# Low parts of the weights by accumulating transfers, and split weights kept from one pass to the next

## The chip, the cores and the metric

The kernel runs on one core of one Trainium2 chip. The metric is the device time in microseconds of one launch, median of several runs. The engines are TensorE (PE; its weight loads are PEld), VectorE (DVE), ScalarE (ACT), GpSimd (POOL) and SyncE (SP), with 16 DMA engines beside them.

## What is computed

One inference step of a two-layer hybrid decoder for a prompt of 1024 tokens and a sample group of 8 x 4 tokens, width 1024, all in float32. Each layer is

```
h    = rmsnorm(x, norm_w[l])
proj = h @ w_in[l]                       # 1024 x 3592, split among four mixers
mixed = concat(s5(...) * silu(g), hgrn2(...) * silu(g), mlstm(...) * silu(g), retention(...) * silu(g))
x    = x + mixed @ w_out[l]
```

with a final RMSNorm. The mixers are recurrences over tokens, computed in chunks. They also return their states.

## The kernel before

The work goes in four passes `n`: layer 0 on the first half of the prompt (pass 0) and on the second half and the sample tokens (pass 1), then layer 1 the same way (passes 2 and 3). Passes 0 and 2 are called even here, 1 and 3 odd. Both passes of a layer use the same weights, and each loads them itself.

In a pass the input projection is cut into 14 blocks of 256 columns of `w_in` (one has 264), listed in `BLOCKS`: seven of kind `ch`, with channels on the partitions of the result, and seven of kind `tok`, with tokens there. A block of kind `tok` has four pieces of 128 tokens (an odd pass has a fifth for the 32 sample tokens, the tiled piece); a block of kind `ch` has two pieces of 128 channels by 512 tokens, or four of 256 or 288 tokens in odd passes. TensorE accumulates a piece in one of three banks of PSUM over eight row tiles `kt`.

A float32 product is made of three in the faster type `fp32r`: the normalised rows are held as `hhi` + `hlo`, the weights as `whi` + `wlo`, and `hhi*whi + hhi*wlo + hlo*whi` is summed (L2384 for `ch`, L2389 for `tok`, one `kt` after the other). The tiled sample piece takes the raw weights instead (L2376). The output projection (L2718, and L2696 in the last pass) takes them raw too.

The weights come so. A block is loaded to `wraw`, which has two slots, from ScalarE's queue (`load_until`, L1250). ScalarE copies it to `whi`, which rounds it (`split_high`, L1233, one instruction of 128 x 2048). GpSimd subtracts, `wlo = wraw - whi` (`split_low`, L1189, eight instructions of 128 x 256, one for each `kt`), and TensorE waits for `whi_done` once and for `wlo_done` at each `kt` of the block's first piece. `whi` and `wlo` have two slots: ScalarE and GpSimd wait for the last piece of the block two before.

Each engine runs the same plan, a list of steps from `make_plan`, in its order, so each is an in-order queue. How the projection steps lie among the steps of the mixers is written out in `PLACES`. `split_after` says behind which step the split of the next block stands: the first piece of the block before it. GpSimd's other work is small: the row scale of the norm (`power`, L1198 and L1200) and that of the head norm (`rs`, L1211 and L1214, a `pow`), which VectorE waits for at L2304. ScalarE also evicts most pieces from PSUM and makes the exponentials of the mixers (L1504). VectorE makes the level tables of the HGRN2 mixer (`hg`) in L2097, L2110 and L2118. The tables of the S5 mixer are made in steps `s5set` on VectorE during the first projections. SyncE's queue issues all other transfers.

Of the kernel before, what the change touches and what calls it, by code (L numbers as in the profile page):

```python
# [25 lines left out]
P = 128  # L26
# [372 lines left out]
def trunk_kernel(nc, inp, out, parts=("hg", "ml", "rt", "s5")):  # L399
    plan = make_plan(parts)  # L400
    ctx = ExitStack()
    with ctx:
# [45 lines left out]
        bank_of = {k: i % 3 for i, k in enumerate(proj_uses)}  # L448
        wslot = {k: i % 2 for i, k in enumerate(w_loads)}
# [72 lines left out]
        wraw = sb("wraw", [P, 2, KT, WC])  # L522
        with nc.sbuf_tensor("tail_w", [P, 2, KT, WC], F32) as tail_w:
            pass
        whi = sb("whi", [P, 2, KT, WC], F32R)
        wlo = sb("wlo", [P, 2, KT, WC], F32R)
# [171 lines left out]
        def tail_weights(b):  # L698
            if b < 2:
                return wraw[:, wslot[(LAST, "wo", b)], :, 0:256]  # L700
            return tail_w[:, hslot[(LAST, ("s5_x", "s5_g")[b - 2])], :, 0:256]
# [27 lines left out]
        whi_done = signal("whi_done", in_blocks)  # L729
        wlo_done = signal("wlo_done", [b + (g,) for b in in_blocks for g in range(KT)])  # L730
# [116 lines left out]
        def split_after(s, part):  # L847


            if s[0] == "norm":  # L850
                return part == 1 and s[1] == 0
            i = None
            if s[0] == "proj" and part == ("mm", pieces_of_block(*s[1:])[0]):
                i = w_loads.index(s[1:]) + 1
            if s[0] == "out" and part[1:] == (3, 1):
                i = w_loads.index((s[1], "wo", 3)) + 1
            return i is not None and i < len(w_loads) and w_loads[i][1] != "wo"
# [33 lines left out]
        def _(sp):  # L891
# [52 lines left out]
            for k in w_loads[:2]:  # L944
                src, width = weight_columns(k)
                sp.dma_start(wraw[:, wslot[k], :, 0:width], src.rearrange("(k p) c -> p k c", p=P)).then_inc(*wr_in[wslot[k]].inc(k))
# [224 lines left out]
        def _(pool):  # L1171
# [49 lines left out]
        def _(act):  # L1221
# [3 lines left out]
            def split_high():  # L1225
# [11 lines left out]
            def load_until(i):  # L1237
                while loads and len(w_loads) - len(loads) <= i:
# [4 lines left out]
                    else:  # L1243
                        act.wait_ge(*whi_done.at(prev))
                        act.wait_ge(*wlo_done.at(prev + (KT - 1,)))
# [4 lines left out]
                    nc.scalar.dma_start(wraw[:, wslot[k], :, 0:width], src.rearrange("(k p) c -> p k c", p=P)).then_inc(*wr_in[wslot[k]].inc(k))  # L1250
# [105 lines left out]
            for s, part in plan:  # L1356
# [13 lines left out]
                if s[0] == "proj" and part == ("mm", pieces_of_block(*s[1:])[0]):  # L1370
                    load_until(w_loads.index(s[1:]) + 1)
                if split_after(s, part):
                    split_high()
                if s[0] == "proj" and part == ("mm", pieces_of_block(*s[1:])[0]):
                    load_until(w_loads.index(s[1:]) + 2)
# [961 lines left out]
        def _(pe):  # L2337
# [6 lines left out]
            for s, part in plan:  # L2344
# [12 lines left out]
                elif s[0] == "proj" and part[0] in ("mm", "mm2"):  # L2357
                    b, n = s[1:], s[1]
                    pe.wait_ge(*whi_done.at(b))
                    sl = hslot[b]  # L2360
                    for k in [part[1]]:
# [8 lines left out]
                        for kt in range(*((0, 4) if part[0] == "mm" else (4, KT)) if long_piece(k) else (KT,)):  # L2370
                            if k == pieces_of_block(*b)[0]:
                                pe.wait_ge(*wlo_done.at(b + (kt,)))
                            if tiled(k):
                                width = BLOCK[b[1]][2] // 4
                                for g in range(4):
                                    mm = nc.tensor.matmul(bank.t[TS * g:TS * g + TS, 0:width], mixT[:, kt, HALF:W], wraw[:, wslot[b], kt, g * width:(g + 1) * width],  # L2376
                                                          start=kt == 0, stop=kt == KT - 1)
                                continue
                            for x, w in ((hhi, whi), (hhi, wlo), (hlo, whi)):
                                first, last = kt == 0 and w is whi and x is hhi, kt == KT - 1 and x is hlo  # L2380
                                if BLOCK[b[1]][3] == "ch":
                                    _, c0, ln = piece_psum(k)
                                    c = slice(c0, c0 + ln)
                                    mm = nc.tensor.matmul(bank.t[:, 0:c.stop - c.start], w[:, sl, kt, k[2] * P:(k[2] + 1) * P], x[:, kt, c],  # L2384
                                                          start=first, stop=last)
                                else:
                                    c = slice(k[2] * P, k[2] * P + P)
                                    width = BLOCK[b[1]][2]
                                    mm = nc.tensor.matmul(bank.t[:, 0:width], x[:, kt, c], w[:, sl, kt, 0:width], start=first, stop=last)  # L2389
                        if kt == KT - 1:  # L2390
# [356 lines left out]
```

## Time and profile before

| | |
|---|---|
| median of 3 runs | 1543.24 us (1541.05 to 1543.25) |
| profiled execution | 1546.32 us, span 1544.5 us |
| mean granted clock of TensorE | 0.934 |
| transfers | 149.84 MB, mean 97 GB/s |
| HBM read, written | 124.42 MB, 23.37 MB |

The span goes from the first to the last instruction of the profiled execution; its own device time is 1546.32 us. Busy times of engines overlap. "Idle before" is the idle time of an engine ahead of a group of instructions, with what ended it.

### The profile page before, as it was taken

The page shows a single profiled execution, that of the slowest core. Times are in us where ns is not written, and L with a number is a line of the kernel's source. Part 1 is how long each engine was busy: PE and PEld are TensorE (multiplying, and loading weights), DVE is VectorE, ACT ScalarE, POOL GpSimd, SP SyncE. Part 2 cuts the span into 40 slices and gives each one's busy share as a digit, 9 for nine tenths or more (in the row PEclk, how much of TensorE's full clock was granted, in tenths as well). Part 3 has the DMA queues.
Part 4 walks back from the last instruction along what each step waited for, and adds up shares of the span by engine and source line. Part 5 has one row for each costly group of instructions (what it writes and reads, how often), then busy time and mean ns, then how long its engine had stood idle before and what let it go on. Part 6 is the DMA issues. An engine that isn't in the chain of part 4 may idle for free.

```text
span 1544.5 us, 31690 instructions
## 1 busy us (share of the span) xinstructions
PE 1376.2 (89%) x12391; PEld 1205.4 (78%) x12391; DVE 889.5 (58%) x2670; ACT 549.8 (36%) x1197; POOL 445.5 (29%) x628
## 2 busy tenths in 40 slices
PE   2868899989898999998999899998999999889896
PEld 2757789778786889876787789987878898779665
DVE  4986746463697535555746543656456444644537
ACT  4435443324333533322452334332642533421011
POOL 4341533522002351432310154352200433331001
PEclk9988999989898999998999999997999999999889
DMA  6322123422233423342322333342313415354501
GB/s 176 96 82 71 55 85 110 130 73 87 59 101 120 130 70 108 102 106 70 113 67 86 113 102 112 109 144 59 114 59 118 111 58 125 137 112 95 148 10 59
DMA packets 167563, 149.84 MB, mean 97 GB/s; under 512 B 63440, under 2 KB 155352, under 8 KB 165752
## 3 DMA queue, kind: packets, MB, share of 16 engines
q1 hardware_dynamic: 96696, 76.38, 17.7%
q10 hardware_dynamic: 70720, 71.44, 15.2%
q8 instruction: 100, 1.64, 0.5%
q14 instruction: 47, 0.39, 0.1%
HBM read 124.42 MB, written 23.37 MB: 96 GB/s over the span
## 4 chain that ended last, share of the span: by engine, by line
PE 64%; DVE 19%; ACT 6%; issue 5%; POOL 3%; DMA 1%; SPq 1%; DVEq 0%; ACTq 0%; POOLq 0%
PE psum L2389 17%; PE psum L2384 16%; PE psum L2718 6%; DVE r L1723 4%; PE psum L2696 3%; PE psum L2637 3%; DVE r L2097 3%; PE psum L2548 2%; PE psum L2636 2%; PE psum L2456 2%; POOL rs L1214 1%; ACT r L1504 1%; POOL wlo L1189 1%; PE psum L2634 1%; DVE QE L2118 1%
## 5 line engine op out<-in xcount | busy, mean ns | idle before, releaser
L1189 POOL TENSOR_TENSOR wlo<-wraw,whi 128x256 fp32r<-128x256 f32 (+1 forms) x448 | 345.9, 807 | 425.9 <-ACT whi L1233 425.9
L2389 PE MATMUL psum<-whi,hhi 128*128 128x256 f32 (+1 forms) x896 | 267.7, 299 | 4.3 <-ACT th L1320 2.0
L2389 PE MATMUL psum<-whi,hlo 128*128 128x256 f32 (+1 forms) x896 | 259.0, 289 | 0.0
L2389 PE MATMUL psum<-wlo,hhi 128*128 128x256 f32 (+1 forms) x896 | 258.6, 289 | 0.0
L2384 PE MATMUL psum<-hhi,whi 128*128 128x288 f32 (+2 forms) x672 | 231.7, 345 | 7.8 <-ACT r L1354 5.6
L2384 PE MATMUL psum<-hhi,wlo 128*128 128x288 f32 (+2 forms) x672 | 220.3, 328 | 0.0
L2384 PE MATMUL psum<-hlo,whi 128*128 128x288 f32 (+2 forms) x672 | 220.3, 328 | 0.0
L2718 PE MATMUL psum<-wraw,mixT 128*128 128x256 f32 x768 | 179.8, 395 | 6.8 <-DVE xo L2314 6.8
L2389 PEld LDWEIGHTS psum<-whi,hhi 128*128 128x128 f32 x896 | 176.9, 197 | 11.1 <-issue 7.0
L2389 PEld LDWEIGHTS psum<-wlo,hhi 128*128 128x128 f32 x896 | 177.0, 198 | 0.7 <-issue 0.5
L1211 POOL TENSOR_SCALAR rs<-mv 128x4 f32<-128x4 f32 (+1 forms) x54 | 10.4, 192 | 575.1 <-DVE mv L2280 574.3
L2389 PEld LDWEIGHTS psum<-whi,hlo 128*128 128x128 f32 x896 | 176.1, 196 | 0.0
L2718 PEld LDWEIGHTS psum<-wraw,mixT 128*128 128x128 f32 x768 | 150.2, 198 | 29.8 <-DVE xo L2314 7.8
L2384 PEld LDWEIGHTS psum<-hhi,whi 128*128 128x128 f32 x672 | 129.7, 193 | 23.3 <-issue 12.4
L1233 ACT ACTIVATE whi<-wraw 128x2048 fp32r<-128x2048 f32 (+1 forms) x56 | 107.3, 1916 | 113.1 <-PE psum L2384 54.2
L2384 PEld LDWEIGHTS psum<-hhi,wlo 128*128 128x128 f32 x672 | 129.7, 193 | 12.4 <-issue 3.4
L2384 PEld LDWEIGHTS psum<-hlo,whi 128*128 128x128 f32 x672 | 129.2, 192 | 10.3
L2277 DVE BATCH_NORM_STATS2 stats<-psum 128x6 f32<-128x64 f32 (+1 forms) x144 | 22.3, 217 | 99.0 <-PE psum L2637 98.9
L2637 PE MATMUL psum<-r,ST 128*128 128x64 f32 (+1 forms) x384 | 70.0, 286 | 2.2 <-issue 2.2
L2097 DVE TENSOR_TENSOR r<-r 128x256 f32<-128x256 f32 (+1 forms) x134 | 53.0, 467 | 15.5 <-PE psum L2548 15.4
L2637 PEld LDWEIGHTS psum<-r,ST 128*128 128x128 f32 x384 | 58.4, 203 | 4.0 <-issue 3.7
L1214 POOL TENSOR_TENSOR rs<-rs,epow 128x4 f32<-128x4 f32 (+1 forms) x54 | 56.7, 1050 | 4.5
(355 smaller groups left out, 2298.6 us busy)
## 6 DMA issues: line engine op xcount, KB each, us to landing
wraw<-in_w_in ACTq DMA_DIRECT2D x50, 1024.0 KB, 5.4
wraw<-in_w_out ACTq DMA_DIRECT2D x14, 1024.0 KB, 5.5
x<-xo SPq DMA_DIRECT2D x48, 128.0 KB, 2.3
r<-x SPq DMA_DIRECT2D x10, 512.0 KB, 5.4
r<-in_c_rot SPq DMA_DIRECT2D x4, 1088.0 KB, 7.2
wraw<-in_w_in ACTq DMA_DIRECT2D x4, 1056.0 KB, 5.9
r<-WTm SPq DMA_DIRECT2D x4, 1024.0 KB, 11.9
r<-VTm SPq DMA_DIRECT2D x4, 1024.0 KB, 5.9
```

The lines of the kernel that those rows point to most:

```text
L1189: nc.gpsimd.tensor_tensor(wlo[:, hslot[b], ks, 0:width], wraw[:, wslot[b], ks, 0:width], whi[:, hslot[b], ks, 0:width].bitcast(F32), ALU.s ...
L1214: nc.gpsimd.tensor_tensor(rs[0:T, :], rs[0:T, :], epow[0:T, :], ALU.pow).then_inc(*rs_done.inc(s))
L1233: nc.scalar.activation(whi[:, hslot[b], :, 0:width], wraw[:, wslot[b], :, 0:width], ACT.Copy).then_inc(*whi_done.inc(b))
L1723: nc.vector.tensor_tensor(o, a, b, op).then_inc(*dve_done.inc())
L2097: nc.vector.tensor_tensor(e, x, x[:, :, at - 1:at].broadcast_to([P, 2 * T // blk, blk]), ALU.subtract).then_inc(*(dve_done.inc() if w else ...
L2384: mm = nc.tensor.matmul(bank.t[:, 0:c.stop - c.start], w[:, sl, kt, k[2] * P:(k[2] + 1) * P], x[:, kt, c], start=first, stop=last)
L2389: mm = nc.tensor.matmul(bank.t[:, 0:width], x[:, kt, c], w[:, sl, kt, 0:width], start=first, stop=last)
L2456: yield nc.tensor.matmul(out(q, a), X(h, ri, q), V_rows(s[1], h, ri, q)[:, v], start=False, stop=ri == 1)
L2548: return nc.tensor.matmul(o.rearrange("p (a x) -> p a x", a=2), E[:, i, k0:k0 + kn], QE[:, i, :, q0:q0 + qn], start=True, stop=True)
L2637: mm = nc.tensor.matmul(o, stt[0:T, h, 0:T], v(h), start=br == "ml", stop=True)
L2696: mm = nc.tensor.matmul(bank.t[r * g:r * g + r, 0:w], x, wo[:, kt, g * w:(g + 1) * w], start=kt == kts[0], stop=kt == kts[-1])
L2718: mm = nc.tensor.matmul(bank.t[0:r, 0:256], mixT[:, row, k[2] * P:k[2] * P + r], wraw[:, wslot[b], kt, 0:256], start=kt == 0, stop=kt == 7)
```

## The change

`split_low` on GpSimd no longer subtracts. In passes 0 and 2 ScalarE writes the negated, rounded weights into `wlo` in two halves (four `kt` each), then the copy into `whi`. GpSimd then issues, for each half, a transfer from `wraw` to `wlo` that adds to what lies there, so that `wlo` becomes `wraw - whi`. For the block before, it first issues two transfers that store its `wlo` and `whi` to memory (`kept_rows`). In passes 1 and 3 nothing is split: ScalarE's queue loads `whi` and `wlo` from those copies at the place where it made the split. Blocks of kind `ch` are not loaded raw there at all (`w_loads` is filtered); those of kind `tok` still are, for the sample piece. `wraw`, `whi` and `wlo` are laid out flat for each slot, so that the columns of a block of any width lie without gaps (`weights`). In the first three-product piece of a block (the first half of it, where it is a long one) TensorE takes all products with `whi` first, and then those with `wlo`.

```diff
+        all_loads = w_loads
+        w_loads = [k for k in all_loads if k[1] == "wo" or k[0] % 2 == 0 or BLOCK[k[1]][3] == "tok"]
...
+        split = [b for b in in_blocks if b[0] % 2 == 0]
+        def whi_ready(b):
+            return whi_done.at(b) if b in split else hi_in[hslot[b]].at(b)
+        def wlo_ready(b, kt):
+            return wlo_sum[hslot[b], kt * 2 // KT].at(b) if b in split else lo_in[hslot[b]].at(b)
+        def weight_half(b, h):
+            width = BLOCK[b[1]][2]
+            return slice(h * KT // 2 * width, (h + 1) * KT // 2 * width)
...
             def split_low():
                 b = blocks.pop(0)
-                prev = before(in_blocks, b, 2)
-                if prev is not None:
-                    pool.wait_ge(*PB[bank_of[last_piece[prev]]].full.at(last_piece[prev]))
-                pool.wait_ge(*whi_done.at(b))
-                width = BLOCK[b[1]][2]
-                for g in range(KT):
-                    ks = slice(g, g + 1)
-                    nc.gpsimd.tensor_tensor(wlo[:, hslot[b], ks, 0:width], wraw[:, wslot[b], ks, 0:width],
-                                            whi[:, hslot[b], ks, 0:width].bitcast(F32), ALU.subtract).then_inc(*wlo_done.inc(b + (g,)))
+                prev = before(in_blocks, b)
+                if prev in split:
+                    pool.wait_ge(*whi_done.at(prev))
+                    for h in range(2):
+                        pool.wait_ge(*wlo_sum[hslot[prev], h].at(prev))
+                    c = slice(0, KT * BLOCK[prev[1]][2])
+                    nc.gpsimd.dma_start(kept_rows("lo", prev), wlo[:, hslot[prev], c].bitcast(F32)).then_inc(*lo_kept[hslot[prev]].inc(prev))
+                    nc.gpsimd.dma_start(kept_rows("hi", prev), whi[:, hslot[prev], c].bitcast(F32)).then_inc(*hi_kept[hslot[prev]].inc(prev))
+                if b not in split:
+                    return
+                for h in range(2):
+                    c = weight_half(b, h)
+                    pool.wait_ge(*wneg_done.at(b + (h,)))
+                    nc.gpsimd.dma_start(wlo[:, hslot[b], c].bitcast(F32), wraw[:, wslot[b], c], accum_op=ALU.add).then_inc(*wlo_sum[hslot[b], h].inc(b))
...
             def split_high():
...
+                if prev in split:
+                    act.wait_ge(*lo_kept[hslot[prev]].at(prev))
+                    act.wait_ge(*hi_kept[hslot[prev]].at(prev))
+                if b not in split:
+                    old = (b[0] - 1, b[1])
+                    c = slice(0, KT * BLOCK[b[1]][2])
+                    act.wait_ge(*hi_kept[hslot[old]].at(old))
+                    nc.scalar.dma_start(whi[:, hslot[b], c].bitcast(F32), kept_rows("hi", b)).then_inc(*hi_in[hslot[b]].inc(b))
+                    act.wait_ge(*lo_kept[hslot[old]].at(old))
+                    nc.scalar.dma_start(wlo[:, hslot[b], c].bitcast(F32), kept_rows("lo", b)).then_inc(*lo_in[hslot[b]].inc(b))
+                    return
                 act.wait_ge(*wr_in[wslot[b]].at(b))
-                width = BLOCK[b[1]][2]
-                nc.scalar.activation(whi[:, hslot[b], :, 0:width], wraw[:, wslot[b], :, 0:width], ACT.Copy).then_inc(*whi_done.inc(b))
+                for h in range(2):
+                    c = weight_half(b, h)
+                    nc.scalar.activation(wlo[:, hslot[b], c], wraw[:, wslot[b], c], ACT.Copy, scale=-1.0).then_inc(*wneg_done.inc(b + (h,)))
+                c = slice(0, KT * BLOCK[b[1]][2])
+                nc.scalar.activation(whi[:, hslot[b], c], wraw[:, wslot[b], c], ACT.Copy).then_inc(*whi_done.inc(b))
...
+                            new = k == [q for q in pieces_of_block(*b) if not tiled(q)][0]
+                            three = ((hhi, whi), (hhi, wlo), (hlo, whi))
+                            order = [(kt, x, w) for kt in kts for x, w in three]
+                            if new:
+                                order = [o for o in order if o[2] is whi] + [o for o in order if o[2] is wlo]
+                            for kt, x, w in order:
+                                if new and w is wlo:
+                                    pe.wait_ge(*wlo_ready(b, kt))
```

`load_until` waits for `wlo_sum` of the block two before instead of `wlo_done`, where that block was split.

## Rows read from the trace of the kernel before

**Rows 1.** The page, busy us (share of the span) and instructions of each engine.

```profile
PE 1376.2 (89%) x12391; PEld 1205.4 (78%) x12391; DVE 889.5 (58%) x2670; ACT 549.8 (36%) x1197; POOL 445.5 (29%) x628
```

**Rows 2.** The page, chain that ended last: share of the span by engine.

```profile
PE 64%; DVE 19%; ACT 6%; issue 5%; POOL 3%; DMA 1%; SPq 1%; DVEq 0%; ACTq 0%; POOLq 0%
```

**Rows 3.** The page, groups: busy us, mean ns | idle before, releaser.

```profile
L1189 POOL TENSOR_TENSOR wlo<-wraw,whi 128x256 fp32r<-128x256 f32 (+1 forms) x448 | 345.9, 807 | 425.9 <-ACT whi L1233 425.9
...
L1233 ACT ACTIVATE whi<-wraw 128x2048 fp32r<-128x2048 f32 (+1 forms) x56 | 107.3, 1916 | 113.1 <-PE psum L2384 54.2
```

**Rows 4.** Waits: total us, times, longest us.

```profile
DVE y L2304 <- POOL rs L1214: 41.3, 52, 10.5
...
ACT whi L1233 <- DMA wraw<-in_w_in: 38.7, 5, 10.0
...
PE psum L2376 <- POOL wlo L1189: 1.7, 4, 0.5
...
PE psum L2389 <- POOL wlo L1189: 0.9, 2, 0.6
```

**Rows 5.** Timeline, 116 to 184 us: start us, us, engine, line [idle before <-releaser].

```profile
120.38 2.77 DVE L2097 TENSOR_TENSOR r<-r 128x256 f32<-128x256 f32 x8 [5.52 <-PE psum L2548]
...
130.62 6.15 POOL L1189 TENSOR_TENSOR wlo<-wraw,whi 128x256 fp32r<-128x256 f32 x8 [36.79 <-ACT whi L1233]
...
132.22 4.69 DVE L2110 TENSOR_TENSOR r<-r 128x128 f32<-128x128 f32 x7
...
166.42 6.89 POOL L1189 TENSOR_TENSOR wlo<-wraw,whi 128x256 fp32r<-128x256 f32 x8
...
167.36 6.57 DVE L2097 TENSOR_TENSOR r<-r 128x256 f32<-128x256 f32 x8
...
178.31 1.50 DVE L2110 TENSOR_TENSOR r<-r 128x128 f32<-128x128 f32 x7
...
179.57 0.66 PE L2636 MATMUL psum<-S_hg,ex 128*128 128x64 f32 x2 [3.99 <-ACT ST L1532]
```

**Rows 6.** Timeline, 19 to 37 us, GpSimd and TensorE.

```profile
24.07 6.51 POOL L1189 TENSOR_TENSOR wlo<-wraw,whi 128x256 fp32r<-128x256 f32 x8 [1.94 <-ACT whi L1233]
30.67 0.19 POOL L1198 TENSOR_SCALAR rstd<-ssq 128x1 f32<-128x1 f32 x1
...
32.95 1.97 PE L2354 MATMUL psum<-const,r 128*128 128x128 f32 x8 [5.02 <-DVE r L1621]
```

**Rows 7.** Windows: stretch, busy us of each engine, PEclk, DMA share, GB/s; last row: L1189.

```profile
40.00:112.00 72.00, 52.03 (x332) 45.84 (x331) 64.69 (x155) 30.11 (x42) 30.05 (x32) 0.90 0.28 92
112.00:200.00 88.00, 76.14 (x797) 67.07 (x798) 56.29 (x165) 39.84 (x78) 28.82 (x38) 0.87 0.21 56
...
906.00:1045.00 139.00, 137.52 (x937) 121.63 (x938) 69.31 (x216) 53.03 (x127) 68.83 (x96) 1.00 0.36 117
147.00:312.00 165.00, 154.15 (x1164) 135.88 (x1163) 94.14 (x288) 67.20 (x149) 69.07 (x98) 0.95 0.32 98
...
40.00:112.00 72.00, 30.05 (x32) 0.90 0.28 92
```

**Rows 8.** Windows: two us in which 8 KB rows were loaded.

```profile
258.00:260.00 2.00, 2.00 (x20) 2.00 (x19) 1.83 (x10) 0.00 (x0) 0.00 (x0) 1.00 1.03 415
```

**Rows 9.** Transfers: a queue's packets, MB, share; issues, KB each, us to landing.

```profile
q10 hardware_dynamic: 70720, 71.44, 15.2%
...
r<-x SPq DMA_DIRECT2D x10, 512.0 KB, 5.4
...
hq<-x SPq DMA_DIRECT2D x2, 512.0 KB, 10.6
```

**Rows 10.** Timeline of ScalarE, 150 to 164 us; last row: chain, start us, us.

```profile
152.39 1.91 ACT L1233 ACTIVATE whi<-wraw 128x2048 fp32r<-128x2048 f32 x1
...
161.54 1.92 ACT L1233 ACTIVATE whi<-wraw 128x2048 fp32r<-128x2048 f32 x1 [5.27 <-PE psum L2384]
161.60 0.37 ACTq L1250 DMA_DIRECT2D wraw<-in_w_in  x1
...
937.79 14.20 PE psum L2389 x120
```

More of the change, by code:

```diff
@@ L521, in trunk_kernel, with weights @@
         hlo = sb("hlo", [P, KT, W], F32R)
-        wraw = sb("wraw", [P, 2, KT, WC])
-        with nc.sbuf_tensor("tail_w", [P, 2, KT, WC], F32) as tail_w:
-            pass
-        whi = sb("whi", [P, 2, KT, WC], F32R)
-        wlo = sb("wlo", [P, 2, KT, WC], F32R)
+        wraw = sb("wraw", [P, 2, KT * WC])
+        with nc.sbuf_tensor("tail_w", [P, 2, KT * WC], F32) as tail_w:
+            pass
+        whi = sb("whi", [P, 2, KT * WC], F32R)
+        wlo = sb("wlo", [P, 2, KT * WC], F32R)
+        def weights(buf, slot, width=256):
+            return buf[:, slot, 0:KT * width].rearrange("p (k c) -> p k c", k=KT)
         mixT = sb("mixT", [P, 10, W])
@@ L699, in tail_weights @@
             if b < 2:
-                return wraw[:, wslot[(LAST, "wo", b)], :, 0:256]
-            return tail_w[:, hslot[(LAST, ("s5_x", "s5_g")[b - 2])], :, 0:256]
+                return weights(wraw, wslot[(LAST, "wo", b)])
+            return weights(tail_w, hslot[(LAST, ("s5_x", "s5_g")[b - 2])])
         def x_rows(x, n, t):
@@ L945, in _ @@
                 src, width = weight_columns(k)
-                sp.dma_start(wraw[:, wslot[k], :, 0:width], src.rearrange("(k p) c -> p k c", p=P)).then_inc(*wr_in[wslot[k]].inc(k))
+                sp.dma_start(weights(wraw, wslot[k], width), src.rearrange("(k p) c -> p k c", p=P)).then_inc(*wr_in[wslot[k]].inc(k))
             def permuted(ap, t):
@@ L1243, in load_until @@
                     else:
-                        act.wait_ge(*whi_done.at(prev))
-                        act.wait_ge(*wlo_done.at(prev + (KT - 1,)))
+                        if prev in split:
+                            act.wait_ge(*whi_done.at(prev))
+                            for h in range(2):
+                                act.wait_ge(*wlo_sum[hslot[prev], h].at(prev))
                         sample = prev + (NCH,)
@@ L2358, in _ @@
                     b, n = s[1:], s[1]
[L2359 removed]
+                    pe.wait_ge(*whi_ready(b))
                     sl = hslot[b]
@@ L2369, in _ @@
                                     pe.wait_ge(*PB[bank_of[u]].free.at(u))
[L2370 to L2374, printed above, removed]
+                        kts = range(*((0, 4) if part[0] == "mm" else (4, KT)) if long_piece(k) else (KT,))
@@ L2375, in _ @@
+                        width = BLOCK[b[1]][2]
+                        if tiled(k):
+                            width //= 4
+                            pe.wait_ge(*wr_in[wslot[b]].at(b))
+                            for kt in kts:
                                 for g in range(4):
-                                    mm = nc.tensor.matmul(bank.t[TS * g:TS * g + TS, 0:width], mixT[:, kt, HALF:W], wraw[:, wslot[b], kt, g * width:(g + 1) * width],
+                                    mm = nc.tensor.matmul(bank.t[TS * g:TS * g + TS, 0:width], mixT[:, kt, HALF:W], weights(wraw, wslot[b], 4 * width)[:, kt, g * width:(g + 1) * width],
@@ L2377, in _ @@
                                                           start=kt == 0, stop=kt == KT - 1)
-                                continue
-                            for x, w in ((hhi, whi), (hhi, wlo), (hlo, whi)):
-                                first, last = kt == 0 and w is whi and x is hhi, kt == KT - 1 and x is hlo
+                        else:
+                            new = k == [q for q in pieces_of_block(*b) if not tiled(q)][0]
[6 more added lines that the diff above has]
+                                    pe.wait_ge(*wlo_ready(b, kt))
+                                first, last = kt == 0 and w is whi and x is hhi, (kt, x, w) == order[-1] and kt == KT - 1
+                                wv = weights(w, sl, width)
@@ L2390, in _ @@
-                        if kt == KT - 1:
+                                    mm = nc.tensor.matmul(bank.t[:, 0:ln], wv[:, kt, k[2] * P:(k[2] + 1) * P], x[:, kt, c0:c0 + ln], start=first, stop=last)
+                                else:
+                                    mm = nc.tensor.matmul(bank.t[:, 0:width], x[:, kt, k[2] * P:k[2] * P + P], wv[:, kt, :], start=first, stop=last)
+                        if kts[-1] == KT - 1:
                             mm.then_inc(*bank.full.inc(k))
```

34 lines of the change are left out of this document (18 added, 16 removed).

## The prediction

> **What bounds the kernel now.** I read the busy line of the page first: TensorE is busy for 1376.2 us of a span of 1544.5 us, VectorE for 889.5, ScalarE for 549.8 and GpSimd for 445.5 [rows 1]. So at most 168 us can be won without touching a matmul, and the change touches none: their number, their shapes and their operands stay. The chain of work that ended last says who fills those 168 us: TensorE 64%, VectorE 19%, ScalarE 6%, GpSimd 3% and transfers 1% of the span [rows 2]. Then the groups: GpSimd makes the low parts in 448 subtractions, 345.9 us, and ScalarE the high parts in 56 copies, 107.3 us [rows 3]. That could suggest that TensorE waits for low parts. The waits say that it doesn't: its three-product matmuls waited 0.9 us for them, in 2 waits, and the small sample pieces, which wait at the same place, 1.7 [rows 4]. Taking the subtraction away can't pay as a wait of TensorE. What it can pay stands in the next view.
>
> **The subtraction slows VectorE.** In the timeline, eight L2097 instructions take 2.77 us together when GpSimd is idle, and the same eight take 6.57 us inside GpSimd's 6.89 us of subtracting; seven L2110 take 1.50 us alone and 4.69 us beside it [rows 5]. The matmul behind the second case then waits 3.99 us at 179.57. The Trainium skill has this in "SBUF — State Buffer", section "Who interferes with whom": a VectorE instruction with two SBUF inputs contends with a GpSimd one that reads SBUF. [...]
>
> **The change part by part.** Terms are against the profiled execution, 1546.3 us (span 1544.5), which lies 3.1 us above the median of 1543.2; I carry the difference over to the median.
>
> (1) *Removed: 448 subtractions.* The slowing is worth on VectorE about: 345.9 us of subtraction times VectorE's busy share of 58% gives 200 us overlapped; if two thirds of that are two-input instructions, whose time doubles, half of 133, 66 us, is excess. Only what lies on the path counts, and I place it by stretches. From 40 to 112 us TensorE is idle for 20 of 72 us, VectorE is busy for 64.7 and the subtraction for 30.05 [rows 7]: overlap 30.05 x 0.9 = 27, excess by the same ratio 9, and the stretch is a VectorE chain (the S5 tables), so -9. From 112 to 200 us the two cases of rows 5 alone are 3.8 + 3.2 us, and a third like the second (L2110 at 156) brings it to 10; TensorE is idle for 12 of 88 us there, so -8. In the rest, 66 - 9 - 10 = 47 us of excess lies mostly beside full TensorE work (137.5 of 139 us from 906 to 1045); about one eighth counts, -6. Ends for the three: 0 (each gap is closed by another engine just behind) and -35 (VectorE's third of the chain, 298 of 889 us, of 66 is 22; half as much again because the excess is thick where VectorE leads).
>
> (2) *GpSimd's own queue.* At the start the subtraction from 24.07 to 30.58 stands ahead of the row scale that the third and fourth tile of the norm wait for, and TensorE idles 5.02 us at 32.95 [rows 6]. Now GpSimd only waits for the negation and issues; ScalarE's square sum comes 2 us later behind the longer split. -3, ends 0 and -5. Later, VectorE waits 41.3 us for `rs` in 52 waits, 0.8 us each, which is the pow itself; the longest is 10.5 us [rows 4]. Nothing is taken for it.
>
> (3) *ScalarE.* In passes 0 and 2 each of 28 blocks has a negation in two halves and then the copy: twice 1916 ns [rows 3], +54 us, of which ScalarE's share on the path is a sixth (6% of 1544 over 550), +9. In passes 1 and 3 the 28 copies of 1916 ns go, -9 by the same share; two issues of 0.37 us come for each [rows 10], and part of the 38.7 us of waiting for raw weights [rows 4] goes. Net +1; ends -9 (odd passes gain, the even ones are covered by TensorE) and +27 (half of 54 on the path, rival three). `whi` is ready 2 us later in even passes. The shortest lead that I find is 152.39 to 161.54 [rows 10]: 9 us from the split's start to the end of the block before. 3.9 us fit, cost 0.
>
> (4) *Low parts by transfer, even passes.* After 1.0 and 1.9 us of negation the halves are issued. No accumulating transfer and none from GpSimd is in the trace, so bounds: a plain 512 KB load lands after 5.4 us in the median, one took 10.6 [rows 9]. With 5.4, the halves land at +6.4 and +8.6 (the second 1.3 us or more behind, sharing the engines). They also queue behind the 2 MiB of stores of the block before, which GpSimd issues just ahead: 5.1 us of work at 410 GB/s [rows 8], of which I take 3 as left, so +12. TensorE needs them when it begins the block plus 1.9 us, as 16 products with `whi` now come first (120 matmuls take 14.20 us, rows 10, so 16 take 1.9). A block of 96 matmuls gives 11.4 us of lead; four blocks have 8 to 10. Late: about 2.4 + 1.4 + 0.5 + 0.3, less some cover, +3. Ends 0 and +80 (two halves of 10.6 us in turn: arrival at +20, late by 5 us or so in 16 dense blocks).
>
> (5) *Transfer capacity.* The full rate is 415 GB/s, at a share of 1.03 [rows 8]: 2.6 us for 1 MiB. Per even block come 2 MiB of stores, 5.1 us, and 1 MiB of accumulation, which costs 2.6 us as a plain transfer and 5.1 us if source and destination are both read. Where it is tightest, 906 to 1045 us, the share is 0.36 of 139 us [rows 7], 50 us, and nine blocks are multiplied: 50 + 9 x (7.7 to 10.2) = 119 to 142 of 139 us. That is at the edge. I take +8 for that stretch, where TensorE has no idle time to give. From 147 to 312 it is 53 + 69 to 92 of 165, which fits. Ends 0 and +50. The odd passes load 2 MiB per block (28 times 5.1) and drop 14 of the loads, which cost 15.2% of 1544.5 us / 68 = 3.5 us each [rows 9]: some 47 us more in each pass, which fits; the copies lie in memory for a pass already, so nothing is late. The short transfers of SyncE (residual blocks, S5 states) lie on 1% of the chain [rows 2], 15 us; a quarter longer in busier queues, +4, ends 0 and +15.
>
> The Trainium skill says in "Collectives: The Full Stack", section "The bandwidth ceiling", that a reducing transfer needs two source reads and so moves at half rate; no run here shows it. By it the stretch needs 142 of 139 us and the slower rival is the likelier one. By its rule for plain transfers ("DMA: Bandwidth & Descriptors", "Anatomy of one DMA": 2.0 us plus bytes over 436 GB/s) a half would land in 3.2 us, where the row has 5.4, and term 4 would be nothing.
>
> (6) The flat layout of `wraw`, `whi`, `wlo` moves the same elements; 0.
>
> Sum: -9 -8 -6 -3 +1 +3 +8 +4 = -10: 1536 in the profiled execution's terms, 1533 for the median.
>
> **Rivals.**
> *Nothing is late.* Terms 3 to 5 are 0 and the release of VectorE is at its far end: 1543 - 35 = 1508. For it: the subtraction overlaps VectorE's longest chains and a full clock may follow from fewer gaps (PEclk is 0.87 in the stretch 112 to 200 and 1.00 from 906 to 1045, rows 7). Against: in even passes ScalarE and GpSimd both keep work of this kind at the head of their queues.
> *Transfers become the bound (the other side).* In even passes each dense block takes as long as its transfers: own weights 3.5, stores 5.1, others 2.1 (50 less nine loads of 3.5, over nine), and the accumulation. The block time in 906 to 1045 is 139/9 = 15.4 us, so it decides from 15.4 - 10.7 = 4.7 us for an accumulated MiB on, 2.4 per half; at 10 us it is +5.3 x 9 = 48, and about +20 more in the first pass (18.3 us per block, plus late weights): 1543 - 26 + 68 = 1585. For it: stores and accumulation share one queue in order. Against: the share is 0.32 to 0.36 now even where blocks are densest [rows 7].
> *The longer split holds ScalarE's queue.* Behind it stand the evictions that free TensorE's banks and the exponentials of the chunks; it now also waits for the stores of two blocks before. At half of 54 us on the path, and the other terms as above: 1533 + 26 = 1559; with covered odd-pass gains about 1550.
> *It doesn't do what it says*: were the low parts to come no sooner but VectorE free, TensorE would show waits of its own on `wlo`; that is the second rival's trace.
>
> **Chances.** Forecast 0.40, its own range 1518 to 1542; nothing late 0.14; transfers 0.30; ScalarE 0.16. Less than 0.2% (3 us), about what a measurement can tell, counts as the same: the upper edge of the forecast and the lower of the ScalarE case give 0.10. Faster 0.50, slower 0.40. The range goes from 1503 to 1590: below lies part of the full release, above an accumulation slower than 10 us per MiB.
>
> **What would show it.** Right: L2097 and L2110 near their undisturbed 0.35 and 0.21 us throughout; no idle of 5 us at 32.95; stretch 40 to 200 shorter by 15 us or more; ScalarE's busy time about unchanged; TensorE's waits on `wlo` transfers under 5 us in all; DMA share near 0.6. Wrong: waits of TensorE on an accumulated low part of several us per block, 14 to 28 times; GpSimd idle on the landing of a sum; ScalarE waiting for a kept copy; a stretch like 906 to 1045 that takes 160 us.

## The result, and the profile after

| | before | after |
|---|---|---|
| median, us | 1543.24 (1541.05 to 1549.28, 4 runs) | 1565.68 (1564.42 to 1570.94, 4 runs) |
| ratio | | 1.0146, 95% interval 1.0108 to 1.0183 |
| profiled execution, us (its span) | 1546.3 (1544.5) | 1570.9 (1569.1) |

The change makes the kernel 22 us slower. I had forecast 1533, faster. The direction was wrong; the time lies between the forecast and the rival in which transfers become the bound (1585).

The page of the changed kernel: busy time of each engine, two DMA queues (packets, MB, share of 16 engines' span), and the chain that ended last by engine.

```profile
PE 1383.4 (88%) x12391; PEld 1214.3 (77%) x12391; DVE 816.4 (52%) x2670; ACT 552.1 (35%) x1225; POOL 182.8 (12%) x292
...
q10 hardware_dynamic: 64224, 115.61, 22.3%
q0 software_dynamic: 16128, 88.28, 18.9%
...
PE 53%; DMA 21%; DVE 11%; ACT 6%; issue 4%; SPq 3%; POOL 2%; ACTq 0%; DVEq 0%; POOLq 0%
```

VectorE lost 73 us of work (889.5 in [rows 1]) and its share of the chain fell from 19% to 11% [rows 2]: the release came. Transfers went from 1% of the chain to 21%. A new queue, q0, is GpSimd's.

The same four stretches as in [rows 7] (PEclk, DMA share and GB/s at the end); 200 to 320 us stands in for 147 to 312.

```profile
40.00:112.00 72.00, 53.68 (x330) 48.23 (x330) 48.71 (x142) 36.13 (x48) 9.78 (x14) 0.85 0.97 285
112.00:200.00 88.00, 83.15 (x892) 74.48 (x887) 47.48 (x182) 55.82 (x95) 18.44 (x26) 0.93 0.74 211
200.00:320.00 120.00, 101.78 (x678) 88.57 (x679) 62.98 (x197) 45.47 (x114) 26.68 (x42) 0.94 0.80 252
906.00:1045.00 139.00, 127.13 (x930) 113.43 (x929) 53.43 (x183) 64.56 (x135) 33.06 (x48) 0.95 0.89 271
```

The DMA share in even passes went from 0.2 to 0.4 up to 0.74 to 0.97. From 906 to 1045 us TensorE was busy for 137.5 of 139 us [rows 7] and is now for 127.1.

Where the time goes shows when the start of each block's first matmul is set against the trace before (after minus before, us; both from the profiled executions, and blocks are named as in the program, in their order):

| first matmul of | difference | what changed since the line above |
|---|---|---|
| pass 0, hg_f | -3.1 | the start: the row scale comes sooner |
| pass 0, hg_q | +9.4 | a raw load lands late, and hg_i waits for its low part |
| pass 0, ml_ifg | -3.0 | VectorE released |
| pass 0, s5_g | -14.5 | VectorE released |
| pass 1, hg_f | -7.1 | change of pass, +7.4 |
| pass 1, ml_q | +5.0 | one stall at 502 us, +8.9, and +3.2 ahead of it |
| pass 2, ml_q | +3.0 | |
| pass 2, ml_o | +14.6 | ml_v waits for its low part, +10.7 |
| pass 2, s5_g | +17.9 | +4.3 in ml_o |
| pass 3, hg_f | +25.8 | change of pass, +7.9 |
| pass 3, s5_g | +23.0 | |

No single wait: five steps of 7 to 12 us, all but one in even passes or at their end. The waits of the changed kernel (us in total, times, longest) name the first kind.

```profile
POOL kept_lo L1221 <- DMA wlo<-wraw: 228.7, 21, 16.7
...
ACT wlo L1283 <- DMA wraw<-in_w_in: 55.4, 9, 12.9
...
PE psum L2448 <- DMA wlo<-wraw: 26.2, 12, 6.4
...
DVE r L1762 <- DMA Tm<-r: 17.6, 2, 15.3
```

TensorE waits 26 us for sums, where it waited 0.9 us for subtractions [rows 4]. The issues with KB each and median us from issue to landing:

```profile
wraw<-in_w_in ACTq DMA_DIRECT2D x36, 1024.0 KB, 10.7
wlo<-wraw POOLq DMA_DIRECT2D x52, 512.0 KB, 12.6
kept_lo<-wlo POOLq DMA_DIRECT2D x26, 1024.0 KB, 8.4
kept_hi<-whi POOLq DMA_DIRECT2D x26, 1024.0 KB, 10.4
```

A sum of 512 KB lands 12.6 us after its issue; I had counted 12 us from the start of the split, which is some 10 us from the issue of the second half. GpSimd's timeline in a dense stretch of pass 2 says how these fit together (start us, us, line, idle before):

```profile
926.10 0.56 POOL L1221 DMA_DIRECT2D kept_lo<-wlo  x1 [13.87 <-DMA wlo<-wraw]
926.65 0.55 POOL L1222 DMA_DIRECT2D kept_hi<-whi  x1
927.23 1.77 POOL L1228 DMA_DIRECT2D wlo<-wraw  x2
...
946.48 0.62 POOL L1221 DMA_DIRECT2D kept_lo<-wlo  x1 [16.11 <-DMA wlo<-wraw]
...
963.54 0.56 POOL L1221 DMA_DIRECT2D kept_lo<-wlo  x1 [14.05 <-DMA wlo<-wraw]
...
980.76 0.56 POOL L1221 DMA_DIRECT2D kept_lo<-wlo  x1 [14.29 <-DMA wlo<-wraw]
```

This is a loop: GpSimd waits for the sums of one block, issues that block's 2 MiB of stores and, right behind them, the sums of the next, and these land only after the stores. One turn takes 20.4, 17.1 and 17.2 us; a block there took 15.4 us before, in the mean of nine. Two of the turns by themselves (DMA share and GB/s at the end):

```profile
946.48:963.54 17.06, 14.77 (x108) 14.18 (x108) 6.40 (x13) 9.74 (x14) 3.01 (x4) 0.89 0.84 247
963.54:980.76 17.22, 16.94 (x117) 15.82 (x116) 1.97 (x6) 7.61 (x22) 2.90 (x5) 0.90 0.83 245
```

So some 14 of the 17 us are work of the 16 engines, and the other 3 are mostly the gap between the last packets of a sum and the first packets of the transfers behind it. TensorE loses time only where its own block is shorter than the turn: from the start of ml_v to that of ml_o it took 12.3 us before and now 22.9, from there to rt_qk 14.5 and now 18.8. The four blocks behind them took 16 to 20 us before, about as long as a turn or longer, and lost nothing.

The second kind are transfers of other queues that became slow. The longest of them in the chain of waits (start us, us):

```profile
34.39 21.31 DMA wraw<-in_w_in
...
58.22 13.27 DMA wlo<-wraw
...
291.97 12.24 DMA ud<-r
...
502.24 13.64 DMA Tm<-r
...
1054.98 11.67 DMA ud<-r
```

`ud<-r` is SyncE's store of the input of the S5 mixer at the end of passes 0 and 2; the row loads of the next pass stand behind it in SyncE's queue. It landed after 4.6 us before (median of the two). The same chain shows another wait just ahead of it: ScalarE, which evicts the pieces that `ud<-r` stores, stands in its queue until a sum lands.

```profile
ACT r L1404 <- DMA wlo<-wraw: 14.2, 2, 7.3
```

The step of 7 to 8 us at each of these changes of pass goes through both. e3 below, without sums, has `ud<-r` as slow at the first change (12.64 us) and steps of only 2.6 and 3.9 us there, so the slow store alone doesn't explain them.

### The profile page after: what moved, and what is told of

It is laid out like the page before. It is cut to its first block, busy times and chain, and to the rows that moved or that the text cites. A ratio compares the mean times of both kernels' runs of the same rounds, so it can differ in the third digit from the quotient of the medians.

```text
span 1569.1 us, 31384 instructions
## 1 busy us (share of the span) xinstructions
PE 1383.4 (88%) x12391; PEld 1214.3 (77%) x12391; DVE 816.4 (52%) x2670; ACT 552.1 (35%) x1225; POOL 182.8 (12%) x292
## 3 DMA queue, kind: packets, MB, share of 16 engines
q1 hardware_dynamic: 96696, 76.38, 17.2%
## 4 chain that ended last, share of the span: by engine, by line
PE 53%; DMA 21%; DVE 11%; ACT 6%; issue 4%; SPq 3%; POOL 2%; ACTq 0%; DVEq 0%; POOLq 0%
PE psum L2448 13%; DMA wlo<-wraw 13%; PE psum L2446 11%; PE psum L2777 6%; PE psum L2755 3%; DMA ud<-r 2%; DMA wraw<-in_w_in 2%; PE psum L2696 2%; PE psum L2607 2%; DVE r L2151 2%; PE psum L2515 2%; PE psum L2693 1%; ACT r L1558 1%; SPq L1043 1%; DVE QE L2172 1%
## 5 line engine op out<-in xcount | busy, mean ns | idle before, releaser
L2448 PE MATMUL psum<-wlo,hhi 128*128 128x256 f32 (+1 forms) x896 | 235.1, 298 | 26.2 <-DMA wlo<-wraw 26.2
L2446 PE MATMUL psum<-hhi,whi 128*128 128x288 f32 (+2 forms) x672 | 226.2, 343 | 1.9 <-DVE hlo L1752 1.5
L2446 PE MATMUL psum<-hlo,whi 128*128 128x288 f32 (+2 forms) x672 | 215.3, 326 | 0.0
L2448 PEld LDWEIGHTS psum<-whi,hhi 128*128 128x128 f32 x896 | 181.4, 202 | 19.4 <-issue 17.2
L2448 PEld LDWEIGHTS psum<-wlo,hhi 128*128 128x128 f32 x896 | 167.7, 203 | 29.3 <-DMA wlo<-wraw 28.8
L2446 PE MATMUL psum<-hhi,wlo 128*128 128x288 f32 (+2 forms) x672 | 188.5, 325 | 1.9 <-DMA wlo<-wraw 1.7
L2448 PEld LDWEIGHTS psum<-whi,hlo 128*128 128x128 f32 x896 | 181.5, 203 | 3.2 <-issue 3.0
L2446 PEld LDWEIGHTS psum<-hhi,wlo 128*128 128x128 f32 x672 | 119.8, 189 | 13.8 <-DMA wlo<-wraw 3.2
L1283 ACT ACTIVATE wlo<-wraw 128x1024 fp32r<-128x1024 f32 (+1 forms) x56 | 56.2, 1051 | 74.3 <-DMA wraw<-in_w_in 55.4
L1228 POOL DMA_DIRECT2D wlo<-wraw x56 | 50.6, 991 | 65.2 <-ACT wlo L1283 64.5
L2151 DVE TENSOR_TENSOR r<-r 128x256 f32<-128x256 f32 (+1 forms) x134 | 45.3, 410 | 19.4 <-PE psum L2607 19.3
## 6 DMA issues: line engine op xcount, KB each, us to landing
wraw<-in_w_in ACTq DMA_DIRECT2D x36, 1024.0 KB, 10.7
wlo<-wraw POOLq DMA_DIRECT2D x52, 512.0 KB, 12.6
```

What stands on the lines that cost most here:

```text
L1228: nc.gpsimd.dma_start(wlo[:, hslot[b], c].bitcast(F32), wraw[:, wslot[b], c], accum_op=ALU.add).then_inc(*wlo_sum[hslot[b], h].inc(b))
L1283: nc.scalar.activation(wlo[:, hslot[b], c], wraw[:, wslot[b], c], ACT.Copy, scale=-1.0).then_inc(*wneg_done.inc(b + (h,)))
L2151: nc.vector.tensor_tensor(e, x, x[:, :, at - 1:at].broadcast_to([P, 2 * T // blk, blk]), ALU.subtract).then_inc(*(dve_done.inc() if w else ...
L2446: mm = nc.tensor.matmul(bank.t[:, 0:ln], wv[:, kt, k[2] * P:(k[2] + 1) * P], x[:, kt, c0:c0 + ln], start=first, stop=last)
L2448: mm = nc.tensor.matmul(bank.t[:, 0:width], x[:, kt, k[2] * P:k[2] * P + P], wv[:, kt, :], start=first, stop=last)
```

## The experiments

Differences below are between medians of four executions and more (block starts and rows are those of one profiled execution each); each kernel ran beside the kernel before (1543.25 us for e1 to e4, 1544.55 for e6, e8, e9 and e10, 1544.01 for the rest).

**e1_sums_first.** The changed kernel, with the sums of a block issued ahead of the stores of the block before.

```
-   stores(prev); for h in range(2): wait(wneg_done[b, h]); sum(b, h)
+   for h in range(2): wait(wneg_done[b, h]); sum(b, h)
+   stores(prev)
```

> The changed kernel, but GpSimd issues the two sums of a block ahead of the stores of the block before. Theory A (a sum is late because it stands behind 2 MiB of stores in GpSimd's one queue): the median landing of a half falls from 12.6 us to 9 or less, TensorE's waits on low parts from 28 us to under 8, and the time from 1566 to about 1548 (1543 to 1553); the stalls behind SyncE's transfers at the changes of pass and near 513 us stay. Rival B (the accumulation itself, 5.3 us of engine time per MiB, is what is too slow): waits stay over 20 us, time 1560 or more.

Measured: 1576.91 us, ratio 1.0223 (1.0196 to 1.0250); slower still than the change by 11 us. Its waits and three pieces of its chain:

```profile
ACT wlo L1282 <- DMA kept_hi<-whi: 97.9, 13, 16.5
...
PE psum L2447 <- DMA wlo<-wraw: 5.3, 5, 1.7
```

```profile
925.68 12.35 DMA kept_hi<-whi
...
941.78 14.60 DMA kept_hi<-whi
...
960.11 12.75 DMA kept_hi<-whi
```

The sums land in 7.7 us and TensorE hardly waits for them, as the theory of the sums' place in the queue had it, and yet nothing is won: the negation of a block writes into the slot from which the stores of two blocks before still read, and ScalarE waits for these 97.9 us. The order only moves the wait. That theory falls as the cause of the 22 us, and so does its rival, slow sums, by which TensorE would have waited over 20 us (the time is where that rival put it). What remains is the amount of traffic, which the next runs vary.

**e2_sums_alone.** No copies: negation and sums in all four passes, raw weights loaded in all.

```
-   split = [b for b in in_blocks if b[0] % 2 == 0]
+   split = list(in_blocks)        # no stores, no loads of copies
```

> No copies in memory: all four passes load raw weights and make the low parts by negation and two accumulating transfers. Theory A (the 2 MiB of stores per block delay the sums, and stores and loads of copies delay SyncE's short transfers, 24 us in three places): halves land after 8 us, waits on low parts under 8 us, none of the three stalls, VectorE free in all passes: 1528 (1520 to 1538). Rival C (the longer split on ScalarE, now in all passes, is what costs): 1545 or more, with ScalarE busy for 605 us and TensorE's banks freed late. Rival B (accumulation too slow): waits on low parts over 20 us, 1550.

Measured: 1526.65 us, 0.9896 (0.9876 to 0.9915), faster than before. Its queue of sums, its loads of weights, the landing of a half, and TensorE's wait:

```profile
q0 software_dynamic: 16128, 58.86, 20.0%
q10 hardware_dynamic: 70720, 71.44, 15.7%
```

```profile
wlo<-wraw POOLq DMA_DIRECT2D x104, 512.0 KB, 8.3
...
wraw<-in_w_in ACTq DMA_DIRECT2D x50, 1024.0 KB, 6.5
```

```profile
PE psum L2435 <- DMA wlo<-wraw: 7.6, 2, 6.7
```

This is within the 1520 to 1538 of the first theory. Sums without stores cost TensorE 7.6 us of waiting in 56 blocks. The copies are what made the change slow. By block starts this kernel was 39 us ahead at the start of pass 3 and gave 18 back in that pass, 6.7 of them between the starts of ml_ifg and ml_q: there TensorE waited as long for a low part, until 1178 us, while a raw load from 1166 us on took 13.53 us and held ScalarE.

**e8_stores_alone** is e2 with the stores of passes 0 and 2, never loaded. **e9_loads_alone** is the changed kernel with the stores of two blocks only, whose copies all blocks of passes 1 and 3 load (the weights of those passes are thus not theirs).

```
e8: +  if prev[0] % 2 == 0: stores(prev)
e9: -  if prev in split: stores(prev)
    +  if prev in ((0, "hg_f"), (0, "ml_ifg")): stores(prev)
```

> Sums in all four passes, as in the version without copies (1526.7), and the copies are stored in passes 0 and 2 but never loaded. The copies cost 39 us in the changed kernel. Theory F (the stores are what costs: sums behind them, and SyncE's store of ud at the end of passes 0 and 2): 1550 or more, halves landing after 12 us in passes 0 and 2. Rival G (loading the copies costs): 1535 or less.

> The changed kernel with two blocks stored instead of 28: every block of passes 1 and 3 loads the copy of hg_f (or of ml_ifg, by its width) of pass 0, so its weights are wrong from pass 1 on and the work is the same. Theory F: the even passes run as without copies, only the stall near 513 us (9 us) and smaller ones from the 2 MiB loads stay, and ScalarE's relief in odd passes gives some back: 1530 (1522 to 1538). Rival G: 1550 or more.

Measured: e8 1580.71 us, 1.0253 (1.0203 to 1.0303), 54 above e2. e9 1524.61 us, 0.9884 (0.9838 to 0.9931), 41 below the changed kernel. Both are as theory F had it. Waits of e8, then a wait of e9:

```profile
POOL kept_lo L1221 <- DMA wlo<-wraw: 223.2, 21, 16.6
ACT wlo L1283 <- DMA wraw<-in_w_in: 92.3, 12, 13.8
...
PE psum L2448 <- DMA wlo<-wraw: 33.2, 14, 5.8
```

```profile
DVE r L1766 <- DMA Tm<-r: 17.3, 2, 15.8
```

The stores alone bring back both kinds of step: by block starts +11.9 at hg_q of pass 0, +8.0 and +10.5 at the two changes of pass and +10.6 at ml_o of pass 2. The loads bring one, the stall of `Tm<-r` near 500 us (+10.1). In e9 the stores of the first block alone still make hg_q of pass 0 late by 12.8 us (e2: 3.1), so the stores in all cost about 41 + 10 = 51 us here and 54 in e8. This price holds whatever the stores bring with them: sums that land late as well as slow transfers of other queues. What the loads save in exchange for the raw loads, splits and sums of passes 1 and 3 is small: the changed kernel stands 15 us below e8, and e9 only 2 below e2.

**e11_half_the_stores.** e8 with the high part's store only.

```
-   store(kept_lo, prev)
```

> Sums in all four passes, and after each block of passes 0 and 2 only the high part is stored (1 MiB), never loaded. With both parts stored the time was 1580.7 us, with none 1526.6. Theory A: the loss goes with the bytes that the stores move in front of the sums, so half of them costs about half, 1548 to 1560 us, and the first blocks' wait for the first sum (TensorE's matmul on wlo) about halves from 33 us. Theory B: what costs is that anything stands there at all (the issue, the wait for the block before), so the time stays at 1570 to 1585 us. Theory C: only the second store is past what the queues can carry; the time is 1525 to 1535 us.

Measured: 1547.71 us, 1.0019 (0.9998 to 1.0040), 21 above e2. Its GpSimd timeline at the place shown above:

```profile
924.24 0.56 POOL L1221 DMA_DIRECT2D kept_hi<-whi  x1 [12.20 <-DMA wlo<-wraw]
...
939.16 0.57 POOL L1221 DMA_DIRECT2D kept_hi<-whi  x1 [12.57 <-DMA wlo<-wraw]
```

```profile
PE psum L2446 <- DMA wlo<-wraw: 16.8, 9, 6.6
```

Half the bytes cost 21 of 54 us, just under the 1548 us at which the proportional theory began. The profiled execution was the fastest of ten, 1536.80 us, so the trace shows only about half of these 21 us. In it this turn of GpSimd's loop takes 14.9 us, under the 15.4 us of a block, and the step at ml_o of pass 2 is 1.2 us instead of 10.6 (the next block adds 2.3, and 2.4 in e8). So there, in that execution, it is the second MiB that counts, and the change from pass 0 to 1 is back at the 1.9 us that it is in e2 (8.0 in e8). At hg_q of pass 0 the first MiB costs already: +7.8 us, between e2's 3.1 and e8's 11.9.

**e3_copies_alone.** Even passes split as before (GpSimd subtracts), with stores; odd passes load the copies.

```
-   nc.gpsimd.dma_start(wlo[...], wraw[...], accum_op=ALU.add)
+   for g in range(KT): nc.gpsimd.tensor_tensor(wlo, wraw, whi, ALU.subtract)
```

> Passes 0 and 2 split as before (one copy on ScalarE, eight subtractions on GpSimd), then stores; passes 1 and 3 load the copies. Theory A: the stalls behind SyncE's transfers at the changes of pass and near 513 us are there (+20 or so), the odd passes gain 5 from a free VectorE: 1558 (1550 to 1565), no wait on low parts in even passes. Rival D (copies are harmless, sums are the whole loss): 1538 or less.

Measured: 1569.63 us, 1.0166 (1.0131 to 1.0201). Copies lose without any sum, although half of the subtractions are gone (VectorE 875.2 us busy). It is above the 1550 to 1565 that I expected, and its loss lies elsewhere than I expected it: by block starts 8.8 us at the stall of `Tm<-r` in pass 1, but 2.6 and 3.9 at the two changes of pass, and the rest in small steps. Its queue q0 holds the stores alone:

```profile
q0 software_dynamic: 8064, 58.85, 9.7%
```

The same 58.9 MB took 20.0% of 1523.3 us as sums in e2, 193 GB/s of the 16 engines, and 9.7% of 1566.8 us as stores, 387 GB/s. The sums go in packets of 4 KB and the stores in packets of 8 KB, but that isn't the reason: in the trace of e2 a 4 KB packet took 328 ns (median) in a sum and 159 ns as a plain packet of SyncE's queue.

**e4_no_low_work and e5_written_not_read.** The kernel before without the subtraction (the low parts stay zero), and with two fills of zero in its place for each of the eight parts, so that GpSimd writes and is held but reads nothing. Both leave the low parts' terms out.

```
-   nc.gpsimd.tensor_tensor(wlo, wraw, whi, ALU.subtract)
e4: +  nc.gpsimd.memset(wlo[one column], 0.0)
e5: +  nc.gpsimd.memset(wlo, 0.0); wait; nc.gpsimd.memset(wlo, 0.0)
```

> The kernel before, with the subtraction left out: GpSimd clears the low parts once at the start and writes one column in place of each subtraction. It leaves out the low parts of the weights. It bounds what any way of taking the subtraction from GpSimd can bring. Theory A (the slowing of VectorE is on the path mainly in the first 200 us): 1520 (1512 to 1528), with L2097 and L2110 at their undisturbed times, most of it gained before 300 us. Rival E (other engines close the gaps): 1538 or more.

> The kernel before with GpSimd's subtraction replaced by two fills of zero of the same tile, one after the other, for each of a block's eight parts: GpSimd still writes the tile twice and is held for a comparable time, but reads nothing (the low parts come out as zero, so their terms are left out). Without any low work the kernel took 1486.6 us, 57 below before. Theory A: what slows VectorE beside GpSimd is GpSimd's reading of two operands; with fills VectorE's copy of the pattern of L2097 falls from 0.82 us mean to about 0.35, VectorE is busy about 817 us, and the time is 1485 to 1500 us. Theory B: GpSimd's time in its own queue or any access of its slows VectorE: the copy stays near 0.8, VectorE near 890 us and the time at 1530 us or more.

Measured: e4 1486.60 us, 0.9645 (0.9616 to 0.9674), 57 below before; e5 1493.29 us, 0.9664 (0.9626 to 0.9701), 51 below. e4 is far below the 1512 to 1528 that I expected. The two VectorE groups of [rows 5] by form, first before, then in e5 (busy us, mean ns):

```profile
L2097 DVE TENSOR_TENSOR r<-r 128x256 f32<-128x256 f32 x128 | 52.1, 479 | 15.0 <-PE psum L2548 14.9
...
L2110 DVE TENSOR_TENSOR r<-r 128x128 f32<-128x128 f32 x112 | 34.7, 381 | 0.0
```

```profile
PE 1362.9 (91%) x12391; PEld 1195.7 (80%) x12391; DVE 817.0 (55%) x2670; ACT 549.8 (37%) x1197; POOL 356.8 (24%) x1076
```

```profile
L2097 DVE TENSOR_TENSOR r<-r 128x256 f32<-128x256 f32 x128 | 44.3, 421 | 17.2 <-PE psum L2548 17.0
...
L2110 DVE TENSOR_TENSOR r<-r 128x128 f32<-128x128 f32 x112 | 24.0, 286 | 0.0
```

GpSimd is filling `wlo` for 280 us in e5, and VectorE's 817.0 us are the 816.6 of e4. (The groups' busy time over their number is 0.35 and 0.21 us, the undisturbed times of [rows 5]; the means of one are longer, since records overlap.) It is GpSimd's reading that slows VectorE; its writing and its being busy don't. This agrees with the Trainium skill, "SBUF — State Buffer", "Who interferes with whom", by which a VectorE instruction with two SBUF inputs contends with a GpSimd one that reads SBUF, not with one that only writes it. (My expectation gave 0.82 us as the mean of the slowed copy. That is its time inside a subtraction; over the whole kernel the mean was 0.48.)

One reservation: a third of the matmuls of the input projection are with zeros in these two runs, and their granted clock, 0.938 to 0.952 by execution, is mostly above the 0.929 to 0.942 of the kernel before. Whether the zeros have a part in that was not tested, so 51 to 57 us is what the release brings at most. With real low parts e10 was 40 us ahead at s5_g of pass 1, where e4 was 46, though it pays for the longer split.

**e6_negation_alone.** The kernel before with ScalarE's negation added in passes 0 and 2.

```
+   for h in range(2): nc.scalar.activation(wlo[half h], wraw[half h], ACT.Copy, scale=-1.0)
    nc.scalar.activation(whi, wraw, ACT.Copy)
```

> The kernel before, with ScalarE's negation in two halves ahead of the copy in passes 0 and 2 (GpSimd then overwrites it by its subtraction). It shows what the longer split on ScalarE costs by itself. Theory A: ScalarE has room, the high part is 2 us later: 1548 (1543 to 1553). Rival C (the longer split is on the path): 1560 or more.

Measured: 1557.03 us, 1.0097 (1.0060 to 1.0134), +12.5 us for 53 us more of ScalarE. That lies between the two theories, more than I expected of this run, and is near the +9 of the prediction's term 3. Here GpSimd's subtraction also begins 2 us later, so the number isn't ScalarE's part alone.

**e12_matmul_order.** The kernel before with the changed order of a block's first piece on TensorE.

```
-   for kt in kts: for x, w in three: matmul
+   order = [o for o in order if o[2] is whi] + [o for o in order if o[2] is wlo]
```

> The kernel before with only the changed order of a block's first piece on TensorE: all products with the high weights first, then those with the low ones. The prediction took nothing for it. Theory A: no change, 1541 to 1546 us. Theory B: since the first products no longer wait for GpSimd's first subtraction, some 2 to 6 us are gained, 1537 to 1541 us. Theory C: the order itself costs (the products with one stationary operand are further apart), 1547 to 1555 us.

Measured: 1544.34 us, 1.0002 (0.9989 to 1.0015). It costs and brings nothing, as I had expected.

**e10_sum_then_subtract and e14_sum_two_passes.** No copies; sums in passes 0 to 2 and subtraction in pass 3, and sums in passes 0 and 1 and subtraction in 2 and 3.

```
+   summed = [b for b in split if b[0] < 3]     # e14: b[0] < 2
```

> Sums and no copies in passes 0 to 2, and in pass 3 the split of before: one copy on ScalarE and eight subtractions on GpSimd. The version with sums throughout gained 39 us up to pass 3 and gave 18 back in it; the kernel without low work gained only 3 in pass 3. If the give-back is the sums' own (a raw load that took 13.5 us, negation ahead of evictions): 1510 (1504 to 1516). If it is something else in the order of the plan: 1525.

> Sums in passes 0 and 1, GpSimd's subtraction in passes 2 and 3, no copies. With sums in three passes the time was 1512.95 us, in four 1526.6, in none 1543. Theory A: the sums help wherever VectorE is what TensorE waits for, in passes 0 to 2, and do harm only in pass 3; without them in pass 2 part of the gain is lost, 1516 to 1526 us. Theory B: ScalarE's longer split costs about what VectorE's release brings after pass 1, so the time is 1506 to 1514 us.

Measured: e10 1512.95 us, 0.9804 (0.9771 to 0.9838), so what e2 gave back in pass 3 came with the sums and the longer split there; e14 1509.59 us, 0.9769 (0.9746 to 0.9792), as its theory B had it, so the gain is all in passes 0 and 1: by block starts e14 is 38 us ahead at s5_g of pass 1 and about 33 from then on. The two are 3 us apart and their intervals overlap. Either beats both kernels.

## Why the prediction was wrong

The sign was wrong because of the transfers, term 5 above all and term 4 with it, which I had at +15 us together and the runs at 61 to 64 (stores 51 to 54, loads 10). The mechanism that I had for the gain was right, and I had it at less than half its size, an error the other way.

*Term 1, VectorE's release: -23 forecast, -51 to -57 measured* (e5, e4, with the reservation above). The excess itself was well estimated, 66 us against 73 measured. What failed is how it was spread and what of it I let count: -9 from 40 to 112 us, -8 from there to 200, and an eighth of the remainder, -6. By block starts e4 gained 17 us in the first stretch, 12 in the second and 23 in the rest of the kernel. VectorE held 19% of the chain [rows 2], but 70 to 80% of its excess (51 to 57 of 73 us) came back as time, if all of the 51 to 57 is its release. That its slowed work lies just where TensorE waits for it is how I read this; I did not follow each piece.

*Term 2, the start: -3 forecast, -3.1 measured.* Right: TensorE's idle time of 5.02 us there is now 1.61.

*Term 3, ScalarE.* For the even passes +9 forecast, +12.5 measured (e6). The half in the odd passes wasn't isolated. Near in size.

*Term 4, sums late: +3 forecast.* Without copies TensorE waited 7.6 us for sums in twice as many blocks (e2). With them it waited 26.2 + 1.7 us. What I wrote here of the queue was right in kind (sums stand behind 2 MiB of stores) and not far off in the landing itself: I took 3 us as left of the stores, and the sums landed in 12.6 us instead of 8.3. What is missing is that GpSimd issues the stores, and with them the next sums, only when the sums of the block before have landed; it waited 228.7 us for that, and I had no cost for it, only a line among the signs of being wrong.

*Term 5, capacity: +12 forecast with SyncE's short transfers; the stores alone cost +51 to +54* (late sums, term 4, included, since e8 and e9 don't part them), the loads 10. This is the step that failed. I compared bytes with capacity over a stretch of 139 us, found 119 to 142 us and wrote that it was at the edge, and then took +8 of an end of +50. The work was nearly right: 142 us over nine blocks is 15.8 us each, and the turns had some 14 to 17. But the sum over a stretch misses two things. First, a turn has to fit each block and not their mean. Stores, sums and GpSimd's wait for their landing follow one another in one queue, and such a turn takes 17 to 20 us with its gaps, where the shortest blocks took 11 to 15. Second, a share of 0.8 to 0.97 makes the short transfers late that stand on the path: I gave them a quarter of 15 us, and the two steps at the changes of pass alone, in which `ud<-r` has a part, were +7.4 and +7.9. "The odd passes fit, nothing is late" failed once, at `Tm<-r` (+8.9; +10.1 in e9).

The Trainium skill's rule that I cited, in "Collectives: The Full Stack", "The bandwidth ceiling", that a reducing transfer reads two sources and moves at half rate, agrees with the runs here: 193 against 387 GB/s. By it I had written that the slower rival was the likelier, and then gave that rival 0.30 and the forecast 0.40.

The rival "transfers become the bound" had the right place and sign. That its 1585 lies only 19 us from the measured time is partly luck, since its errors have opposite signs. It took 10 us for an accumulated MiB, where 193 GB/s make 5.4; at 5.4 its own rule gives 6 us for the dense stretch and not 48, and 15 were measured (between ml_q and s5_g of pass 2). It had no changes of pass in it, and a release of 26 us in place of 51 to 57. The terms put together from the runs: e4 -57; split and sums about +18 (e9 stands 38 above e4, of which 10 are the stores of its first block and 10 the stall of `Tm<-r`); loads +10; stores +51. That is +22, and 22 were measured, as it must be, since the 18 closes the sum. The release and the stores have runs of their own behind them, and the loads the step in the trace of e9; what part of the 18 is ScalarE's and what the sums' stays open.

## What to carry to other kernels

Where a new transfer enters a queue, compute the turn of that queue: what it must move for one block, one after the other, with the waits for landings in it, against the time of the shortest blocks and not their mean; a capacity summed over a long stretch hides it. When GpSimd's two-input work on SBUF runs beside VectorE chains that TensorE waits for, most of VectorE's excess can be path time, as here. A copy that saves work in one pass is paid for in the pass that writes it (here 51 to 54 us for the stores against 2 to 15 saved); try the replacement without the copy first.

## What the runs showed of the hardware

- An accumulating transfer within SBUF moved 193 GB/s of destination bytes over the 16 engines, a store to memory 387 GB/s. Packets of 4 KB took 328 ns (median) in a sum and 159 ns in a plain transfer (e2). Without stores in the queue a half of 512 KB lands in 8.3 us (median), behind 2 MiB of them in 12.6.
- Each sum holds GpSimd for 0.9 us to issue, each store for 0.55; the 56 sums of 28 blocks are 50.6 us, where the subtractions of 28 blocks took 172.7 (e3).
- GpSimd writing SBUF for 280 us left VectorE's two-input instructions at their undisturbed time (421 and 286 ns); reading two operands raised these to 479 and 381 ns in the mean.
